# Expert matrices laid out with neighbouring rows in a partition, and transposes that read every 8th or 4th column

## The chip, the cores and the metric
The kernel runs on one core of a Trainium2 chip. The metric is the device time in microseconds of one execution; the time before is the median of three runs.

## What is computed
A decoder trunk of two layers on 512 tokens of 1024 features, all in fp32. A layer has a mixer (sliding-window attention and an mLSTM beside each other, from one input projection) and a mixture of 16 experts. The change touches the second part: the shift and scale before the experts, the router and the experts' matrices.

```python
for l in range(DEPTH):                                  # DEPTH = 2
    mod = c_act @ ada_w[l] + ada_b[l]
    sh1, sc1, g1, sh2, sc2, g2 = split(mod, 6)          # 1024 each
    ...                                                 # mixer, x = x + g1 * ...
    h2 = rms_norm(x, norm_ffn_w[l]) * (1.0 + sc2) + sh2
    scores = sigmoid(h2 @ router_w)                     # 16 experts, best group of 4, top 2 in it
    # per expert e, for the tokens routed to it:
    y = (silu(h @ w_gate[l, e]) * (h @ w_up[l, e])) @ w_down[l, e]   # 1024 -> 512 -> 1024
    x = x + g2 * (weighted sum of the two experts of a token)
```

## The kernel before
The five engines run their own instruction streams and meet in semaphores. In the loop over layers TensorE works through a fixed order of products (`group_order`), each into one of two PSUM banks that ScalarE and VectorE empty in turn. Then comes the expert stage.

Tokens are sorted by expert on the chip: their normalised rows are scattered into the DRAM buffer `expert_rows`, in blocks of 64 rows of one expert. The trace shows 22 blocks in layer 0 and 24 in layer 1. For every block b TensorE runs, in this order (loop at line 1199): gate/up products of block b+1 (`gate_up`, line 1160, 16 products in two passes, 32 matmuls); the transposes of the rows of block b+2 (`x_transposes`, line 1152, eight of 64 rows by 128 columns); the down product of block b (`down`, line 1172); the transposes of the hidden rows of block b+1 (`h_transposes`, line 1166, four). A transpose takes the tile `xg` or `hx` as TensorE's stationary operand and the identity as the moving one. ScalarE and VectorE apply scale and shift while they empty the x transposes (lines 800 and 1685, one value a partition from `A2` and `modc`), and VectorE writes a block's result to `yb` (1689), which ScalarE's queue stores in two DMAs (817).

An expert has 2 MB each of gate, up and down. Three buffers hold them. SyncE issues gate and up of expert e when the last gate/up product of expert e-3 is done (`load_expert`, lines 433 to 436, issues at 428 and 431), GpSimd issues down when its last down product is done (541 to 544). All matrix loads of SyncE go through one queue in order. The source of each is made by `of`: partition p receives rows p, p+128, p+256 and so on, each a run of 2 KB (gate, up) or 4 KB (down) in DRAM. TensorE's product number k takes rows 128k to 128k+127 and so needs in partition p the feature 128k+p; that is what `x_transposes` gives it, by reading columns 128k to 128k+127.

The same feature order serves the router: `h2T` (line 1114) transposes the normalised rows `xn`, `rwz` holds the router's matrix (line 395), `A2` and the columns 24 to 39 of `modc` hold scale and shift. These come from parts 6 to 9 of the `ada` product. For those VectorE sums eight weighted rows (`sum_mid`), and TensorE turns the sum of 512 columns into four PSUM columns (`column_sums`, line 865, called from 1095), between the products of `gb` and `yb`. Norm weight and bias for them are columns of `pc`, a transposed block of small parameters. `params` (lines 368 to 387) loads small parameters with 14 DMAs a layer, for layer 0 at the start ahead of `x` and three parts of `ada_w`, for layer 1 among the loads of layer 0's experts.

## Time and profile before

| | |
|---|---|
| median of 3 runs | 1733.24 us (1731.43 to 1737.04) |
| profiled execution, span from first to last instruction | 1724.8 us |
| TensorE busy | 1506.9 us, 87% of the span |
| VectorE, ScalarE, GpSimd busy | 563.9, 323.4, 121.8 us |
| mean granted clock of TensorE | 0.940 of full speed |
| moved by DMA | 366.59 MB in 160813 packets, mean 213 GB/s |
| queue q1 (SyncE) | 127568 packets, 256.26 MB |
| queue q0 (GpSimd) | 21664 packets, 83.89 MB |
| expert stages | about 540 to 846 us and 1380 to 1700 us |

How to read it: a line number stands for the instruction's line in the kernel. Times of instructions are in us or, where marked, ns; positions are us from the first instruction. PE is TensorE's matmuls, PEld its weight loads, DVE VectorE, ACT ScalarE, POOL GpSimd, SP SyncE; a q behind it means the engine's issuing side. Ends of matmuls are modelled. The DMA share is the mean busy share of the core's 16 DMA engines; it can come out a little above 1.

### The profile page before, as it was taken

What the parts mean: (1) busy time and instruction counts of PE and PEld (TensorE: products, weight loads), DVE (VectorE), ACT (ScalarE), POOL (GpSimd) and SP (SyncE); (2) the same over time, 40 slices, a digit from 0 to 9 for tenths busy, and PEclk for the clock granted to TensorE, in tenths of its full rate; (3) what the DMA queues carried; (4) which work ended last, traced back from release to release, by engine and by line L of the source; (5) the groups of instructions that cost most, each with busy time, mean ns of one, the idle gap of its engine ahead of it and who ended that gap; (6) DMA issues with size and microseconds to landing.
All of it is one profiled execution on the core that took longest, in us unless ns stands there. A gap on an engine that the chain in (4) does not pass through costs nothing.

```text
span 1724.8 us, 18335 instructions
## 1 busy us (share of the span) xinstructions
PE 1506.9 (87%) x5819; PEld 669.3 (39%) x5820; DVE 563.9 (33%) x1459; ACT 323.4 (19%) x809; POOL 121.8 (7%) x157
## 2 busy tenths in 40 slices
PE   4999999999983999987749999999999387999982
PEld 1544444544441333332335444454444132333330
DVE  1346432446333212111134554243642411221213
ACT  3133411200011212111132343111000121221210
POOL 1100000011101000000111000000110100000001
PEclk8999999999996999999769999999999789999996
DMA  9822111055747899999952111113563799997984
GB/s 307 338 97 98 49 49 49 13 206 173 291 142 268 268 375 379 376 388 360 322 180 98 49 49 50 49 49 108 206 224 145 292 314 381 378 354 247 310 303 165
DMA packets 160813, 366.59 MB, mean 213 GB/s; under 512 B 12433, under 2 KB 14705, under 8 KB 160753
## 3 DMA queue, kind: packets, MB, share of 16 engines
q1 hardware_dynamic: 127568, 256.26, 42.2%
q0 software_dynamic: 21664, 83.89, 12.8%
q10 hardware_dynamic: 11520, 25.70, 5.0%
q8 instruction: 31, 0.51, 0.1%
q14 instruction: 30, 0.24, 0.0%
HBM read 334.37 MB, written 31.46 MB: 212 GB/s over the span
## 4 chain that ended last, share of the span: by engine, by line
PE 69%; DMA 11%; SPq 5%; DVE 5%; issue 4%; ACT 2%; POOL 2%; ACTq 0%; DVEq 0%; POOLq 0%; PEldq 0%
PE bank L939 23%; PE bank L1160 14%; PE bank L929 11%; PE bank L1105 6%; PE bank L1172 6%; DMA weight_ring<-in_w_up_dram 6%; DMA regA<-in_w_up_dram 2%; SPq L428 2%; SPq L431 2%; SPq L371 2%; DMA weight_ring<-in_ada_w_dram 1%; PE bank L1152 1%; PE bank L999 1%; POOL expert_rows L558 1%; PE bank L988 1%
## 5 line engine op out<-in xcount | busy, mean ns | idle before, releaser
L939 PE MATMUL bank<-h_features,weight_ring 128*128 128x512 f32 x768 | 342.4, 599 | 3.1 <-ACT regB L674 1.9
L1160 PE MATMUL bank<-weight_ring,merged_features 128*64 128x512 f32 x960 | 227.2, 628 | 35.3 <-DMA weight_ring<-in_w_up_dram 28.2
L939 PEld LDWEIGHTS bank<-h_features,weight_ring 128*128 128x128 f32 x768 | 144.8, 192 | 182.7 <-issue 182.4
L929 PE MATMUL bank<-weight_ring,h_features 128*128 128x512 f32 (+1 forms) x512 | 196.1, 541 | 1.7 <-ACT h_features L628 1.7
L1703 DVE TENSOR_TENSOR merged_features<-bank,merged_features 64x512 f32<-64x512 f32 x44 | 30.5, 693 | 381.8 <-ACT merged_features L809 381.8
L1160 PEld LDWEIGHTS bank<-weight_ring,merged_features 128*64 128x64 f32 x960 | 73.5, 144 | 165.4 <-issue 160.8
L929 PEld LDWEIGHTS bank<-weight_ring,h_features 128*128 128x128 f32 x512 | 96.0, 190 | 97.0 <-issue 91.6
L1160 PE MATMUL bank<-h_features,merged_features 128*64 128x512 f32 x256 | 117.1, 612 | 11.0 <-DMA regA<-in_w_up_dram 10.0
L1160 PE MATMUL bank<-regA,merged_features 128*64 128x512 f32 x256 | 117.5, 614 | 0.0
L1105 PE MATMUL bank<-weight_ring,merged_features 128*128 128x512 f32 x256 | 110.4, 593 | 3.0 <-POOL merged_features L538 3.0
L1172 PE MATMUL bank<-weight_ring,merged_features 128*64 128x512 f32 x480 | 109.6, 598 | 1.6 <-DVE merged_features L1689 1.6
L809 ACT ACTIVATE merged_features<-bank 64x512 f32<-64x512 f32 x46 | 27.1, 589 | 367.9 <-PE bank L1160 367.9
L1152 PE MATMUL bank<-ident,merged_features 64*128 64x64 f32 x384 | 34.9, 233 | 44.5 <-DMA merged_features<-expert_rows 44.5
L800 ACT ACTIVATE merged_features<-bank,mod_cols,scale 128x64 f32<-128x64 f32 x192 | 61.9, 402 | 60.6 <-PE bank L1152 58.3
L1105 PEld LDWEIGHTS bank<-weight_ring,merged_features 128*128 128x128 f32 x256 | 48.5, 190 | 63.4 <-issue 60.2
L1544 DVE SCALAR_TENSOR_TENSOR regP<-weight_ring,c_padded,regP 128x512 f32<-128x512 f32 x84 | 63.2, 752 | 3.0
L1160 PEld LDWEIGHTS bank<-h_features,merged_features 128*64 128x64 f32 x256 | 34.8, 141 | 73.7 <-issue 73.7
L1685 DVE TENSOR_SCALAR merged_features<-bank,scale,mod_cols 128x64 f32<-128x64 f32 x192 | 52.8, 338 | 27.1 <-PE bank L1152 25.5
L1689 DVE TENSOR_TENSOR merged_features<-bank,g_rows 128x512 f32<-128x512 f32 x46 | 31.8, 692 | 89.8 <-PE bank L1172 78.9
L1152 PEld LDWEIGHTS bank<-ident,merged_features 64*128 64x128 f32 x384 | 28.2, 142 | 82.0 <-DMA merged_features<-expert_rows 44.7
L939 PE MATMUL bank<-regB,weight_ring 128*128 128x512 f32 x128 | 57.4, 594 | 1.6 <-DVE regB L1562 1.6
L939 PE MATMUL bank<-regA,weight_ring 128*128 128x512 f32 x128 | 57.6, 592 | 0.0
(304 smaller groups left out, 1376.1 us busy)
## 6 DMA issues: line engine op xcount, KB each, us to landing
weight_ring<-in_ada_w_dram SPq DMA_DIRECT2D x24, 2048.0 KB, 8.7
weight_ring<-in_w_gate_dram SPq DMA_DIRECT2D x22, 2048.0 KB, 21.1
weight_ring<-in_w_down_dram POOLq DMA_DIRECT2D x22, 2048.0 KB, 14.9
weight_ring<-in_w_up_dram SPq DMA_DIRECT2D x22, 2048.0 KB, 20.4
weight_ring<-in_w_in_dram SPq DMA_DIRECT2D x18, 2048.0 KB, 8.9
h_features<-in_w_gate_dram SPq DMA_DIRECT2D x10, 2048.0 KB, 17.4
regA<-in_w_up_dram SPq DMA_DIRECT2D x10, 2048.0 KB, 27.4
regB<-in_w_down_dram POOLq DMA_DIRECT2D x10, 1536.0 KB, 11.5
```

The lines of the kernel that those rows point to most:

```text
L371: sp.dma_start(dst, src).then_inc(params_in, 16)
L428: sp.dma_start(gate_w[p], of(w_gate, l, e)).then_inc(w_gu[p], 16)
L431: sp.dma_start(up_w[p], of(w_up, l, e)).then_inc(w_gu[p], 16)
L800: last = ac.activation(xT[:, k, :], ps[2][:, MB * k:MB * k + MB], ACT.Identity, scale=A2[:, k:k + 1], bias=modc[:, 24 + k:25 + k])
L929: ins = te.matmul(bank[:, 0:w], hT[:, k, P * i:P * i + P], wv[:, k, :], start=(k == 0), stop=(k == KD - 1))
L939: ins = te.matmul(bank[:, :], wv[:, k, c0:c0 + P], rhs[:, k, :], start=(k == 0), stop=(k == kn - 1))
L1105: ins = te.matmul(bank[:, :], merged[:, k, P * i:P * i + P], slot("wo", k // 4, 4, D)[:, k % 4, 512 * h:512 * h + 512], start=(k == 0), st ...
L1152: ins = te.transpose(ps[(2, 6)[k % 2]][:, MB * k:MB * k + MB], xg[p][:, P * k:P * k + P], ident[MB * p:MB * p + MB, MB * p:MB * p + MB])
L1160: ins = te.matmul(ps[3][64 * part:64 * part + 64, :], xT[:, k, :], w[:, k, :], start=(k == 0), stop=(k == KD - 1))
L1172: ins = te.matmul(ps[5][64 * half:64 * half + 64, :], hxT[:, k, :], down_w[p][k][:, 512 * half:512 * half + 512], start=(k == 0), stop=(k ...
L1544: link(ve.scalar_tensor_tensor(mid_sum, w[:, k, :], cz[:, k, 0:1], mid_sum, ALU.mult, ALU.add))
L1685: last = ve.tensor_scalar(xT[:, k, :], ps[6][:, MB * k:MB * k + MB], A2[:, k:k + 1], modc[:, 24 + k:25 + k], ALU.mult, ALU.add)
```

## The change
Partition p of an expert's gate and up tile now holds rows 8p to 8p+7, one run of 16 KB in DRAM, and of a down tile rows 4p to 4p+3, also 16 KB (for the third buffer 12 KB and 4 KB). Product k then takes the feature 8p+k (4p+k) in partition p. So the x transposes read columns k, k+8, k+16 and so on, and the hidden ones k, k+4 and so on. The scale and shift columns, the router's matrix and `h2T` follow the same order of features. Their parameters come straight from DRAM into a new tile `ffc` with three more small DMAs a layer, in runs of 32 bytes, and `column_sums_ffn` makes a part's sum with eight products of 64 columns (read with a step of 8) in place of four of 128.

```diff
+        ffc = sb("ffn_param_cols", [P, 3, KD])
...
-            return w.rearrange("l e (k p) f -> (l e) p k f", p=P)[bass.ds(l * E + e, 1)].rearrange("a p k f -> p (a k) f")
+            return w.rearrange("l e (p k) f -> (l e) p k f", p=P)[bass.ds(l * E + e, 1)].rearrange("a p k f -> p (a k) f")
...
+                rows(ffc[:, 0, :], lay(norm_ffn_w, l).rearrange("a (p k) -> p (a k)", p=P))
+                rows(ffc[:, 1, :], lay(ada_b, l)[:, 3 * D:4 * D].rearrange("a (p k) -> p (a k)", p=P))
+                rows(ffc[:, 2, :], lay(ada_b, l)[:, 4 * D:5 * D].rearrange("a (p k) -> p (a k)", p=P))
...
-            sp.dma_start(rwz[:, :, 0:E], router_w.rearrange("(k p) e -> p k e", p=P)).then_inc(const_in, 16)
+            sp.dma_start(rwz[:, :, 0:E], router_w.rearrange("(p k) e -> p k e", p=P)).then_inc(const_in, 16)
...
-                wait_head(pe, params_in, t, 14 * 16, 14 * 16)
+                wait_head(pe, params_in, t, 17 * 16, 17 * 16)
...
+            def column_sums_ffn(bank, rows, h):
+
+                for k in range(KD):
+                    ins = te.matmul(bank[64 * h:64 * h + 64, k:k + 1], rows.rearrange("q (p k) -> q k p", k=KD)[:, k, :], ones[:, 0:1], start=True, stop=True)
+                return ins
...
-                            ins = column_sums(bank, mid_sum)
+                            ins = column_sums_ffn(bank, mid_sum, c_ % 2)
...
-                        ins = te.transpose(bank[:, P * i:P * i + P], xn[:, i, P * k:P * k + P], ident[:, :])
+                        ins = te.transpose(bank[:, P * i:P * i + P], xn[:, i, :].rearrange("t (p k) -> t k p", k=KD)[:, k, :], ident[:, :])
...
-                        ins = te.transpose(ps[(2, 6)[k % 2]][:, MB * k:MB * k + MB], xg[p][:, P * k:P * k + P],
+                        ins = te.transpose(ps[(2, 6)[k % 2]][:, MB * k:MB * k + MB], xg[p].rearrange("t (p k) -> t k p", k=KD)[:, k, :],
...
-                        ins = te.transpose(ps[4][:, MB * k:MB * k + MB], hx[:, P * k:P * k + P], ident[0:MB, 0:MB])
+                        ins = te.transpose(ps[4][:, MB * k:MB * k + MB], hx.rearrange("t (p k) -> t k p", k=FC)[:, k, :], ident[0:MB, 0:MB])
...
-                        columns(j, bank, read, link)
+                        r, c0 = 64 * (j % 2), 24 if j < 8 else 32
+                        link(ve.tensor_copy(modc[r:r + 64, c0:c0 + KD], bank[r:r + 64, 0:KD]))
+                        ve.sem_inc(read, 1)
...
-                        link(ve.tensor_tensor(modc[:, 24:40], modc[:, 24:40], pc[:, 84:100], ALU.add))
-                        link(ve.scalar_tensor_tensor(A2[:, :], modc[:, 32:40], 1.0, pc[:, 8:16], ALU.add, ALU.mult))
+                        link(ve.tensor_tensor(modc[:, 24:40], modc[:, 24:40], ffc[:, 1:3, :].rearrange("p a k -> p (a k)"), ALU.add))
+                        link(ve.scalar_tensor_tensor(A2[:, :], modc[:, 32:40], 1.0, ffc[:, 0, :], ALU.add, ALU.mult))
```

## Rows read from the trace of the kernel before

**Rows 1.** the page, part 4: shares of the chain that ended last.
```profile
PE 69%; DMA 11%; SPq 5%; DVE 5%; issue 4%; ACT 2%; POOL 2%; ACTq 0%; DVEq 0%; POOLq 0%; PEldq 0%
```

**Rows 2.** TensorE's waits, 540 to 846 us: us in total, times, longest.
```profile
PE bank L1160 <- DMA weight_ring<-in_w_up_dram: 18.5, 3, 11.1
PE bank L1160 <- DMA regA<-in_w_up_dram: 5.6, 2, 4.5
```

**Rows 3.** the same, 1380 to 1700 us.
```profile
PE bank L1160 <- DMA weight_ring<-in_w_up_dram: 9.7, 2, 4.9
PE bank L1160 <- DMA regA<-in_w_up_dram: 4.4, 1, 4.4
```

**Rows 4.** stretches: length, busy us by engine, clock, DMA share, GB/s.
```profile
370.00:376.00 6.00, 6.00 (x15) 2.66 (x14) 3.14 (x4) 0.00 (x0) 2.53 (x2) 1.00 1.05 388
55.00:73.00 18.00, 18.00 (x56) 10.44 (x55) 4.22 (x13) 2.79 (x7) 1.97 (x1) 1.00 1.02 422
590.00:823.00 233.00, 208.44 (x1049) 77.65 (x1049) 44.73 (x108) 40.57 (x108) 11.16 (x16) 0.96 1.04 374
822.90:825.90 3.00, 3.00 (x8) 1.08 (x10) 0.00 (x0) 0.00 (x0) 0.00 (x0) 0.50 1.05 388
1409.00:1459.00 50.00, 40.60 (x202) 15.14 (x199) 9.93 (x24) 8.36 (x23) 3.57 (x5) 0.96 1.04 375
1460.00:1644.00 184.00, 183.58 (x944) 68.63 (x942) 37.72 (x91) 35.03 (x93) 6.35 (x9) 0.99 0.95 326
```

**Rows 5.** the chain in order of time: start, us, what.
```profile
18.35 20.28 DMA weight_ring<-in_ada_w_dram
...
715.64 9.83 PE bank L1160 x32
...
1675.62 9.40 PE bank L1160 x32
```

**Rows 6.** TensorE in order of time, one block of layer 0: start, us.
```profile
578.74 3.65 PE L1172 MATMUL bank<-weight_ring,merged_features 128*64 128x512 f32 x16
582.32 0.46 PE L1166 MATMUL bank<-ident,merged_features 64*128 64x64 f32 x4
582.71 7.09 PE L1160 MATMUL bank<-weight_ring,merged_features 128*64 128x512 f32 x32
589.73 0.71 PE L1152 MATMUL bank<-ident,merged_features 64*128 64x64 f32 x8
```

**Rows 7.** SyncE's issues in order of time: start, us that the issue took.
```profile
8.95 0.43 SPq L371 DMA_DIRECT2D qk_norm_rows<-in_q_norm_w_dram  x1
...
590.12 0.37 SPq L428 DMA_DIRECT2D weight_ring<-in_w_gate_dram  x1
...
760.84 10.65 SPq L428 DMA_DIRECT2D h_features<-in_w_gate_dram  x1
...
799.02 3.45 SPq L428 DMA_DIRECT2D weight_ring<-in_w_gate_dram  x1
...
1643.54 2.73 SPq L431 DMA_DIRECT2D weight_ring<-in_w_up_dram  x1
```

**Rows 8.** TensorE's weight loads in the block of rows 6.
```profile
578.10 0.57 PEld L1152 LDWEIGHTS bank<-ident,merged_features 64*128 64x128 f32 x8 [0.81 <-issue]
```

**Rows 9.** the page, part 5: busy us, mean ns of one.
```profile
L1689 DVE TENSOR_TENSOR merged_features<-bank,g_rows 128x512 f32<-128x512 f32 x46 | 31.8, 692 | 89.8 <-PE bank L1172 78.9
L1152 PEld LDWEIGHTS bank<-ident,merged_features 64*128 64x128 f32 x384 | 28.2, 142 | 82.0 <-DMA merged_features<-expert_rows 44.7
```

**Rows 10.** VectorE by shape, whole run: busy us, mean ns of one.
```profile
L1646 DVE TENSOR_REDUCE gate_weights<-regP 128x4 f32<-128x64 f32 x4 | 0.9, 220 | 0.1
...
L1630 DVE TENSOR_REDUCE regP<-regP 128x16 f32<-128x64 f32 x2 | 0.5, 265 | 0.1
```

**Rows 11.** TensorE in order of time: column sums, and transposes of h2T.
```profile
405.56 0.95 PE L865 MATMUL bank<-ones,regP 128*128 128x1 f32 x8
...
502.20 5.06 PE L1114 MATMUL bank<-ident,regA 128*128 128x128 f32 x24 [2.75 <-DVE regA L1586]
```

**Rows 12.** landing times of the stores of line 817.
```profile
DMA to landing us min/median/max: 2.3/6.3/7.4
```

## The prediction, made before the changed kernel ran

> **What bounds the kernel now.** I read the page's chain first: of what ended last 69% is TensorE and 11% DMA [rows 1]. So TensorE sets the end except where a transfer comes late. Next the list of TensorE's waits, for the two expert stages alone. Five gate/up products of layer 0 wait for `w_up`, 18.5 + 5.6 = 24.1 us [rows 2], and three of layer 1, 9.7 + 4.4 = 14.1 us [rows 3]. A wait leaves a second loss: the granted clock is 0.50 (1.2 GHz) in the 3 us after it [rows 4], and the 32 matmuls that follow take 9.83 or 9.40 us [rows 5] where they take 7.09 in a block that didn't wait [rows 6]. Third, the table by stretches [rows 4]. From 590 to 823 us the DMA engines are busy without a break (share 1.04) at 374 GB/s, and so from 1409 to 1459. From 1460 to 1644 they are not the limit: TensorE is busy 183.6 of 184 us. So layer 0 is bound by its transfers and layer 1, for the longer part, by TensorE. The change touches both: its loads may be faster, its transposes can hardly be.
>
> **Loads with 16 KB runs.** Gate and up are read in 2 KB packets, down in 4 KB packets. The trace has both sizes at a steady rate: 2 KB packets alone (`ada_w`, 370 to 376 us) move 388 GB/s, 4 KB packets alone (the zero fill of the row buffer, in the other direction, 55 to 73 us) 422 GB/s [rows 4]. No row shows 16 KB. The bounds are no gain, and a little above 422 (say 435), since the step from 2 to 4 KB gave 34 GB/s and further ones should give less. I take 422, the nearest row. Of layer 0 twelve experts' gate and up (numbers 4 to 15, issued from 590.12 to 799.02 and after [rows 7]), 12 x 4.19 = 50.3 MB, cross the saturated stretch: 129.6 us at 388, 119.2 us at 422, so 10.4 us less, 0.87 us an expert. Of layer 1 three experts (3, 4, 5) fall in such a stretch, 2.6 us, and the last one's own load gains 0.9.
>
> The sum does not use this: the Trainium skill, page "DMA: Bandwidth & Descriptors", section "Why small descriptors are slow (HBM only)", names a fixed overhead of about 3 cycles a packet. For 2 KB, 64 beats of 32 B, that is an estimated 4.5%, half of the 9% between my two rows; by it layer 0 would gain some 5 us in place of 10.4.
>
> SyncE is freed too: an issue of 1024 packets takes 0.37 us when the ring has room and 10.65 when it is full [rows 7]; one of 128 should stay short. I cost this at nothing. The engines are busy the whole time, so an earlier issue only lengthens the line.
>
> **Transposes with a step.** A transposed tile is TensorE's stationary operand, so what is read with a step is the weight load; the products' own operands stay contiguous. The eight loads of L1152 span 0.57 us [rows 8]; less the last one's own 0.142 [rows 9] that is 0.061 us from one to the next. What does a step of 16 or 32 bytes cost? No TensorE row has one. VectorE has: in the router a reduction over 64 elements in steps of 16 bytes (L1630) takes 265 ns, against 220 over 64 contiguous ones (L1646) [rows 10], 0.70 ns an element more. VectorE's plain rate is 692 ns for 512 elements, 1.35 each [rows 9], so as a ratio this is 1.5 and adds 32 ns to a weight load; as time, 128 x 0.70, it adds 90. The middle is a doubled load, +61 ns, which I take. Ends for the range: 0, and 142 (the whole printed duration once more). The first load of each group can be fetched under the matmuls before it, so 7 + 3 = 10 of a block's 12 are exposed: +0.61 us a block, where a block now takes 7.09 + 3.65 and its transposes some 0.9 [rows 6].
>
> A rule of the Trainium skill, page "SBUF — State Buffer", section "Door 1: The DMA port swizzle", says that memory is read in 16-byte lines and that a step is free up to 4 elements of fp32. By it the eight loads of `xg` (step 8) pay and the four of `hx` (step 4) don't. The VectorE row has a step of exactly 4 and is slower, so the trace speaks against the free step; by the rule a block would pay 0.43 us, and the sum would be some 3 us lower.
>
> **Expert stages, summed.** Layer 0: transfers -10.4. The saturated stretch starts when expert 1's last gate/up product frees its buffer, three blocks in, 3 x 0.61 = +1.8. After the last load has landed the last transposes add 0.4. TensorE's own path up to that landing has 24.1 us of waits and twice 2.7 of slow clock to lose (29.5) and 20 x 0.61 = 12.2 of work to gain, so the transfers still end last. Net **-8.2**. Layer 1: the early stretch -2.6 (TensorE has 4.9 + 4.4 us of slack there and uses 3.7). From 1459 to 1675 there are 18 blocks, +11.0. The last wait (4.8 us, before 1675.62) is for a load issued at 1643.54, when TensorE itself frees the buffer, three blocks earlier; so it shrinks by 0.9 + 1.8 = 2.7. Tail +0.4. Net **+6.1**.
>
> **The other transposes and the sums.** `h2T`: 64 loads over both layers, back to back, 24 in 5.06 us [rows 11]; 56 exposed x 61 ns = **+3.4** (0 to 8.0). `column_sums_ffn` has 8 products where `column_sums` had 4, each in two passes. 8 passes take 0.95 us now [rows 11], 0.119 each. The 16 passes load 64 columns each: half the time of 128 contiguous ones, the same if the step doubles it; so 16 x 0.119 = 1.90, +0.95 us. Nothing covers it (matmuls stand on both sides) and it runs 8 times: **+7.6** (3.7 with a free step).
>
> **Three more parameter loads.** At the start SyncE issues them ahead of `x` and three `ada` parts, and the chain runs along that queue into the load that ends at 38.6 us [rows 5]. 3 x (0.43 + 0.04) = **+1.4** [rows 7]; they move 4 KB each, nothing further. For layer 1 they are issued among the expert loads, long before TensorE asks. The re-laid router and VectorE's copies (8 columns for 4) keep their counts: nothing.
>
> **Sum.** -8.2 + 6.1 + 3.4 + 7.6 + 1.4 = +10.3 us. The profiled execution spans 1724.8 us; the median is 1733.24, so 8.4 us lie outside the span or between executions, and the change doesn't touch them. 1733.2 + 10.3 = **1743.5 us**, +0.6%.
>
> **Rivals.**
> *B, the step is free for TensorE.* For it: a weight load need not be fed as VectorE is. Against it: VectorE's row. Layer 0 -10.4, layer 1 -2.6 - 0.9, the sums +3.7, the start +1.4: -8.8, **1724.4 us**; with 435 GB/s another 5 less, 1719. This is the faster side.
> *C, a load with a step costs its printed 142 ns more.* A block pays 1.42. Layer 0: TensorE's path becomes the later one, -29.5 + 28.4 + 0.8 = -0.3; layer 1 -2.6 + 25.6 - 5.0 + 0.8 = +18.8; `h2T` +8.0, sums +12.9, start +1.4: +40.8, **1774.0 us**.
> *D, small row transfers starve behind 16 KB packets.* At 422 GB/s an engine takes 0.62 us for 16 KB. A store of a block's result is 8 packets an engine; it lands in 6.3 us median, 2.3 at least [rows 12]. If each packet waits for one of each weight queue it takes 8 x 1.24 + 2.3 = 12.2 us. The next result is there 11.7 us after this one and is wanted some 7 us later, so about 18 us are hidden. Only if bursts of eight go first (2 x 10 + 2.3 = 22 us) is TensorE held, up to 5 us a block; in half of layer 1's 18 bound blocks +45 on the forecast, **1789 us**.
> *E, the loads don't get faster.* The engines' share is 1.05 with 2 KB and 1.02 with 4 KB packets, so packets may not be the limit. Layer 0 +2.2, layer 1 +9.6, the rest +12.4: +24.2, **1757.4 us**.
>
> **How the numbers follow.** Forecast (step 32 to 90 ns, loads at 422): chance 0.43, with these ends +1.3 to +19.2, 1734.5 to 1752.4. B 0.26, C 0.10, D 0.05, E 0.11, anything else 0.05. A measurement of this kernel can tell about 0.3%, 5.2 us, from no change. Faster: B and a little of the rest, 0.29. Within: the forecast's low end and B's high end, 0.16. Slower: 0.55. The range takes in B and E and stops short of C: 1716 to 1771.
>
> **What would show it.** TensorE's rows: L1152 x8 grows from 0.71 us to about 1.1, L1166 x4 from 0.46 to 0.65, L865 in mid-layer from 0.95 for x8 to 1.9 for x16. The windows: saturated stretches above 374 GB/s, near 400; packets down from 160813 to about 93000; SyncE's issues of L428 and L431 under 1 us. Wrong would be: L1152 unchanged (B), L1689 or L1172 waiting for row stores (D), an unchanged rate (E).

## The result: slower, by more than forecast

| | before | after |
|---|---|---|
| median | 1732.34 us (4 runs, 1725.11 to 1737.04) | 1757.22 us (4 runs, 1746.71 to 1763.19) |
| ratio | | 1.0143, 95% interval 1.0116 to 1.0169 |
| profiled execution, span | 1724.8 us | 1761.6 us |
| packets of DMA | 160813 | 93325 |
| first gate/up product to last down product, layer 0 | 294.9 us | 293.9 us |
| the same, layer 1 | 308.0 us | 316.7 us |

The change costs 24.9 us; +10.3 was forecast. The direction held, but the cost is 2.4 times the forecast's. The profiled execution of after was the slowest of its four, 6 us above their median. That of before was quicker than its median: in the four executions of after the time is 1.6 us longer than the span, so a span of 1724.8 us stands for some 1726.4 us, 6 below the median. So the spans differ by 36.8 us. Of these 2.8 fall before the end of the first token's products, 7.9 before the first expert stage, -1.0 in it, 15.7 between the stages, 8.7 in the second, 2.7 behind it. In the chain of after there is a wait of 7.0 us between the layers, on work that the trace can't name, which the profiles of e1 to e5 don't have. Of the 15.7 us 4.3 come in that place (from the stage's last product to the next layer's first transposes TensorE takes 44.3 us for 40.0).

**Where the time ends now.** The page's chain of after, shares by engine, then its largest groups:

```profile
PE 72%; DMA 12%; DVE 5%; issue 4%; ACT 3%; POOL 2%; SPq 1%; ACTq 1%; another core or an unknown queue 0%; DVEq 0%; POOLq 0%; PEldq 0%
PE bank L949 23%; PE bank L1170 14%; PE bank L939 11%; DMA expert_rows<-merged_features 9%; PE bank L1182 7%; PE bank L1115 6%; PE bank L1162 2%; PE bank L1176 1%; DMA weight_ring<-in_ada_w_dram 1%; PE bank L1009 1%; POOL expert_rows L562 1%; PE bank L998 1%; DVE x_tokens L1728 1%; DMA expert_rows<-regA,slot_index 1%; SPq L372 1%
```

The DMA share is about that of rows 1, but it is another DMA: the weights are gone, and the stores of the blocks' results (`expert_rows<-merged_features`) hold 9%. TensorE's waits in the two stages of after (total us, times, longest) name no weight any more; rows 2 and 3 had 24.1 and 14.1 us for `w_up`. What they name is the down product (L1182, before L1172), in layer 0 and then in layer 1:

```profile
PE bank L1182 <- issue: 8.8, 3, 4.8
...
PE bank L1182 <- issue: 5.3, 1, 5.3
PE bank L1182 <- DVE merged_features L1701: 4.3, 1, 4.3
```

By the kernel's order it waits for a PSUM bank that VectorE has not emptied, because VectorE waits for its one result buffer; the trace names VectorE in the last of the three rows, and e3 below tests it. VectorE's waits for the stores, whole run, before and after:

```profile
DVE merged_features L1689 <- DMA expert_rows<-merged_features: 11.0, 2, 6.6
```
```profile
DVE merged_features L1701 <- DMA expert_rows<-merged_features: 154.3, 20, 13.8
```

And the chain of after in layer 0, pieces over 1.2 us: six stores in a row, 14.2 us in the mean. All 92 stores of after have a median of 8.6 us and a longest of 17.1, where rows 12 had 6.3 and 7.4:

```profile
695.25 14.74 DMA expert_rows<-merged_features
711.61 15.73 DMA expert_rows<-merged_features
728.97 13.49 DMA expert_rows<-merged_features
744.08 11.06 DMA expert_rows<-merged_features
756.76 13.18 DMA expert_rows<-merged_features
771.57 17.13 DMA expert_rows<-merged_features
```

**The rate.** Stretches of 100 us inside the saturated part of layer 0, before and then after (length; busy us of PE, PEld, DVE, ACT, POOL; clock, DMA share, GB/s):

```profile
600.00:700.00 100.00, 99.70 (x518) 37.21 (x516) 22.22 (x54) 20.25 (x54) 5.58 (x8) 1.00 1.04 379
700.00:800.00 100.00, 87.02 (x420) 31.73 (x416) 17.54 (x43) 15.95 (x43) 5.51 (x8) 0.93 1.05 379
```
```profile
600.00:700.00 100.00, 100.00 (x494) 38.83 (x492) 19.88 (x48) 18.09 (x48) 3.69 (x7) 1.00 1.00 376
700.00:800.00 100.00, 89.66 (x406) 35.80 (x404) 16.71 (x41) 15.82 (x42) 4.22 (x8) 0.91 1.01 389
```

379 GB/s became 376 and 389: 1% more in the mean, not the 9% taken. The landing times moved nevertheless (KB each, median us), gate and up first of before, then of after:

```profile
weight_ring<-in_w_gate_dram SPq DMA_DIRECT2D x22, 2048.0 KB, 21.1
weight_ring<-in_w_down_dram POOLq DMA_DIRECT2D x22, 2048.0 KB, 14.9
weight_ring<-in_w_up_dram SPq DMA_DIRECT2D x22, 2048.0 KB, 20.4
```
```profile
weight_ring<-in_w_down_dram POOLq DMA_DIRECT2D x22, 2048.0 KB, 15.1
weight_ring<-in_w_gate_dram SPq DMA_DIRECT2D x22, 2048.0 KB, 10.9
weight_ring<-in_w_up_dram SPq DMA_DIRECT2D x22, 2048.0 KB, 16.3
```

What gate and up gained, down lost. Counted from the first gate/up product of layer 0, the last `w_up` of that layer landed after 264.8 us in place of 276.5, and the last `w_down` after 276.3 in place of 265.3. The last weights of the layer came no earlier than before.

**The steps.** One block of after in order of time, to lay beside rows 6, and the weight loads of its x transposes, beside rows 8:

```profile
578.47 1.09 PE L1162 MATMUL bank<-ident,merged_features 64*128 64x64 f32 x8
579.50 3.65 PE L1182 MATMUL bank<-weight_ring,merged_features 128*64 128x512 f32 x16
583.08 0.69 PE L1176 MATMUL bank<-ident,merged_features 64*128 64x64 f32 x4
583.70 7.09 PE L1170 MATMUL bank<-weight_ring,merged_features 128*64 128x512 f32 x32
...
578.47 0.96 PEld L1162 LDWEIGHTS bank<-ident,merged_features 64*128 64x128 f32 x8 [0.81 <-issue]
```

0.71 + 0.46 became 1.09 + 0.69: +0.61 us a block, as forecast. The loads are (0.96 - 0.57) / 7 = 0.056 us further apart.

**The column sums.** TensorE in mid-layer of after, then the clock (the column before the DMA share) in the product behind a sum. Rows 11 had 0.95 us for a sum, the product behind it took 7.11:

```profile
420.99 2.08 PE L895 MATMUL bank<-ones,regP 128*64 128x1 f32 x16
423.00 8.83 PE L949 MATMUL bank<-h_features,weight_ring 128*128 128x512 f32 x16
...
423.00:426.00 3.00, 3.00 (x6) 1.49 (x6) 2.63 (x5) 0.00 (x0) 0.29 (x1) 0.66 0.52 132
426.00:429.00 3.00, 3.00 (x6) 1.11 (x5) 2.86 (x5) 0.00 (x0) 0.00 (x0) 0.77 1.04 406
```

### The profile page after: what moved, and what is told of

Same layout as the page of the kernel before. It is cut to its first block, busy times and chain, and to the rows that moved or that the text cites. A ratio compares the mean times of both kernels' runs of the same rounds, so it can differ in the third digit from the quotient of the medians.

```text
span 1761.6 us, 18469 instructions
## 1 busy us (share of the span) xinstructions
PE 1553.5 (88%) x5883; PEld 704.2 (40%) x5884; DVE 557.9 (32%) x1459; ACT 323.1 (18%) x809; POOL 114.5 (6%) x157
## 2 busy tenths in 40 slices
DMA packets 93325, 366.62 MB, mean 208 GB/s; under 512 B 13297, under 2 KB 15569, under 8 KB 80977
## 4 chain that ended last, share of the span: by engine, by line
PE 72%; DMA 12%; DVE 5%; issue 4%; ACT 3%; POOL 2%; SPq 1%; ACTq 1%; another core or an unknown queue 0%; DVEq 0%; POOLq 0%; PEldq 0%
PE bank L949 23%; PE bank L1170 14%; PE bank L939 11%; DMA expert_rows<-merged_features 9%; PE bank L1182 7%; PE bank L1115 6%; PE bank L1162 2%; PE bank L1176 1%; DMA weight_ring<-in_ada_w_dram 1%; PE bank L1009 1%; POOL expert_rows L562 1%; PE bank L998 1%; DVE x_tokens L1728 1%; DMA expert_rows<-regA,slot_index 1%; SPq L372 1%
## 5 line engine op out<-in xcount | busy, mean ns | idle before, releaser
L949 PE MATMUL bank<-h_features,weight_ring 128*128 128x512 f32 x768 | 350.0, 610 | 2.2 <-ACT regB L678 1.9
L1170 PEld LDWEIGHTS bank<-weight_ring,merged_features 128*64 128x64 f32 x960 | 69.6, 141 | 135.4 <-issue 130.5
L1182 PE MATMUL bank<-weight_ring,merged_features 128*64 128x512 f32 x480 | 113.6, 617 | 6.9 <-DVE merged_features L1701 4.3
L1170 PE MATMUL bank<-h_features,merged_features 128*64 128x512 f32 x256 | 113.2, 595 | 1.0 <-issue 1.0
L1170 PE MATMUL bank<-regA,merged_features 128*64 128x512 f32 x256 | 113.3, 595 | 0.0
L1701 DVE TENSOR_TENSOR merged_features<-bank,g_rows 128x512 f32<-128x512 f32 x46 | 31.8, 692 | 210.7 <-DMA expert_rows<-merged_features 154.3
L1162 PE MATMUL bank<-ident,merged_features 64*128 64x64 f32 x384 | 52.6, 279 | 45.6 <-DMA merged_features<-expert_rows 45.6
L1162 PEld LDWEIGHTS bank<-ident,merged_features 64*128 64x128 f32 x384 | 45.9, 200 | 83.1 <-DMA merged_features<-expert_rows 45.7
L1182 PE MATMUL bank<-regB,merged_features 128*64 128x512 f32 x192 | 51.2, 674 | 12.9 <-issue 12.8
## 6 DMA issues: line engine op xcount, KB each, us to landing
regB<-in_w_down_dram POOLq DMA_DIRECT2D x10, 1536.0 KB, 14.1
```

Of the source, the lines that this page charges most:

```text
L949: ins = te.matmul(bank[:, :], wv[:, k, c0:c0 + P], rhs[:, k, :], start=(k == 0), stop=(k == kn - 1))
L1162: ins = te.transpose(ps[(2, 6)[k % 2]][:, MB * k:MB * k + MB], xg[p].rearrange("t (p k) -> t k p", k=KD)[:, k, :], ident[MB * p:MB * p + M ...
L1170: ins = te.matmul(ps[3][64 * part:64 * part + 64, :], xT[:, k, :], w[:, k, :], start=(k == 0), stop=(k == KD - 1))
L1182: ins = te.matmul(ps[5][64 * half:64 * half + 64, :], hxT[:, k, :], down_w[p][k][:, 512 * half:512 * half + 512], start=(k == 0), stop=(k ...
L1701: ve.tensor_tensor(yb, ps[5][:, :], g2bc[:, :], ALU.mult).then_inc(y_taken, 1)
```

## The experiments
**Theory 1**: 16 KB packets move hardly more bytes; they change which queue waits, and starve the row stores; the steps cost 0.61 us a block; the stepped column sums cost their own time and the clock behind them. **Rivals**: rival E of the prediction as it stood (nothing but a rate that stays), the number of passes rather than the step as the price of the sums (3b below), the step alone as the cause, and a plain gain from the loads alone.

Each series had its own runs of the kernel before beside it: 1729.58 us for e1 to e4, 1730.31 for e5 to e8, 1732.05 for e9 to e12, where the runs of after had 1732.34. So a difference between two medians of different series is good to some us only; from the ratios e3, e4, e6 and e8 come out 17, 13, 16 and 33 us below after, for 18, 15, 16 and 37 from the medians.

### e1 and e2: the layout of after, smaller packets

```diff
-                    sp.dma_start(gate_w[p], of(w_gate, l, e)).then_inc(w_gu[p], 16)
+                    for k in range(KD):
+                        sp.dma_start(gate_w[p][:, k:k + 1, :], of(w_gate, l, e)[:, k:k + 1, :]).then_inc(w_gu[p], 16)
```
Up is cut alike, down goes in four DMAs with packets of 4 KB. e2 takes two rows at a time.

> The changed kernel with the same places for every row, but gate and up loaded in eight DMAs of 2 KB packets and down in four of 4 KB packets, as before the change. Theory 1 (the row stores starve behind 16 KB packets): VectorE's wait for row stores before its result row, 154 us in the changed kernel, falls back to about 11 us, no down product waits for it, and the gate/up products wait for w_up again, 35 to 50 us; the expert stages keep a block period of about 12.25 us. Time 1750 to 1760 us, since the transfers bind layer 0 again. Rival (the store path stalls for another reason, such as the longer block): VectorE's wait for stores stays above 100 us. Rival 2 (packet size changes nothing in the rate): the saturated stretch of layer 0 shows the same GB/s as in the changed kernel.

> The changed kernel with gate and up in four DMAs of 4 KB packets each and down in four of 4 KB packets; places unchanged. Theory 1: a store's packet waits for 4 KB per queue and not for 16, VectorE's wait for stores is under 30 us, the stalls of the down products in both layers (some 10 us a layer) are gone; weight waits are smaller than with 2 KB packets because the rate is nearer to 422 GB/s. Time 1740 to 1750 us. Rival (16 KB is better for the weights than it is bad for the rows): 1757 us or more.

e1: 1759.03 us, ratio to before 1.0158 (1.0117 to 1.0199). VectorE's waits for stores 154.3 to 12.1 us, and TensorE waits for `w_up` again, 33.8 us. e2: 1747.44 us, 1.0107 (1.0069 to 1.0145); stores 11.3, `w_up` 22.9. The rate at 600 to 800 us is 370 and 381 in e1, 382 and 385 in e2. So with 2 KB packets the weight waits are back and the store waits gone, as in the kernel before, and the time can't be told from that of after. That the big packets' gain is paid back in full is not shown: in the profiled executions the two stages together take 620.1 us in e1 and 610.6 in after. 4 KB is better than 2 KB (the slowest run of e2, 1753.01, is faster than the fastest of e1, 1756.17); against after its interval overlaps. The fall of the store waits needs smaller packets only, since every row has the place that it has in after.

### e3: two result buffers

```diff
-        yb = mflat[:, 3072:3584]
+        yb = [mflat[:, 3072:3584], mflat[:, 3584:4096]]
...
-                                act.dma_start(xd[bass.ds(b * MB, MB), 512 * h:512 * h + 512], yb[64 * h:64 * h + 64, :]).then_inc(y_out, 16)
+                                act.dma_start(xd[bass.ds(b * MB, MB), 512 * h:512 * h + 512], yb[p][64 * h:64 * h + 64, :]).then_inc(y_fly[p], 16)
```

> The changed kernel with two buffers for a block's result, so that VectorE waits for the store before last and not for the last one. 16 KB packets stay. Theory 1: VectorE's wait for stores almost vanishes, the down products follow without a gap, and each expert stage is some 10 us shorter: 1735 to 1745 us. Rival (the transfers as a whole are the limit, the stores only show it first): the gate/up products wait for w_up in place of that, and the time stays within 5 us of 1757.

1739.04 us, 1.0047 (1.0028 to 1.0066): 18 us less than after. The stage of layer 0 takes 286.8 us (after 293.9, before 294.9), that of layer 1 307.9 (316.7, 308.0).

```profile
DVE merged_features L1705 <- DMA expert_rows<-merged_features: 52.5, 10, 9.5
```

Nothing else was changed, so the late stores behind a single buffer are shown to cost this much. A third of VectorE's wait is left, but TensorE's gaps ahead of down products shrink from 18.4 us in after (8.8 and 9.6 in the two layers) to some 0.6.

### e4 and e6: the steps of xn and of the sums taken away
e4: VectorE writes the normalised rows in the new order, and the x and h2T transposes read without a step.

```diff
-                    ve.tensor_scalar(xn[:, i, :], xs[:, i, :], rs[:, 4 + i:5 + i], None, ALU.mult).then_inc(xn_ready, 1)
+                    ve.tensor_scalar(xn[:, i, :].rearrange("t (k p) -> t k p", k=KD), xs[:, i, :].rearrange("t (p k) -> t k p", k=KD), rs[:, 4 + i:5 + i], None, ALU.mult).then_inc(xn_ready, 1)
```

> The changed kernel, but VectorE writes the normalised rows in the new order of features (reading with a step of 8 there, 8 instructions in all), so that the transposes of xg and h2T read contiguous columns; only the four of hx keep their step. Theory 2 (a stepped weight load costs about 60 ns more): the eight transposes span 0.71 us again, the block period falls from 12.25 to about 11.85 us, and the time by 8 to 13 us to about 1747. Rival (the step is not what lengthened the block): the period stays at 12.25 and the time at 1757. If the stalls for stores depend on the block period, they grow by a part of what is gained.

1741.81 us, 1.0067 (1.0034 to 1.0099), 15 below after by the medians and 13 by the ratios. The block period is 11.87 us for 12.25, as expected, and VectorE's waits for stores grow to 177.4 us.

e6: VectorE's last addition of a column sum is written in the new order (`mid_perm`), and the eight products read it without a step.

```diff
-                    ins = te.matmul(bank[64 * h:64 * h + 64, k:k + 1], rows.rearrange("q (p k) -> q k p", k=KD)[:, k, :], ones[:, 0:1], start=True, stop=True)
+                    ins = te.matmul(bank[64 * h:64 * h + 64, k:k + 1], rows[:, 64 * k:64 * k + 64], ones[:, 0:1], start=True, stop=True)
```

> The changed kernel, but VectorE writes the last step of the weighted sum in the new order (one instruction per part reads with a step), so the eight products of the column sums read contiguous columns; their count stays. Theory 3a (the step lengthens them): 2.08 us fall to about 1.4 us, the clock stays up in the product group after them (7.1 us and not 8.8) and the time falls by 5 to 10 us to 1748 to 1752. Theory 3b (their number does, each pass having a fixed price near 0.12 us): they stay at 1.9 us or more, the clock still falls, and the time stays within 3 us of 1757.

1740.86 us, 1.0052 (1.0029 to 1.0075): 16.4 less than after. A sum of e6 with the product behind it, and its clock:

```profile
422.84 1.09 PE L896 MATMUL bank<-ones,regP 128*64 128x1 f32 x16
423.86 7.13 PE L950 MATMUL bank<-h_features,weight_ring 128*128 128x512 f32 x16
...
424.00:427.00 3.00, 3.00 (x8) 1.32 (x9) 2.78 (x4) 0.00 (x0) 1.14 (x1) 1.00 0.57 150
```

16 passes without a step take 1.09 us, with it 2.08, and the clock stays at 1.00 (2.4 GHz). So it is the step and not the number of passes. (A pass of these sixteen takes 64 columns, one of the eight before 128.)

### e5: down as before

```diff
-                        ins = te.transpose(ps[4][:, MB * k:MB * k + MB], hx.rearrange("t (p k) -> t k p", k=FC)[:, k, :], ident[0:MB, 0:MB])
+                        ins = te.transpose(ps[4][:, MB * k:MB * k + MB], hx[:, P * k:P * k + P], ident[0:MB, 0:MB])
...
-                        po.dma_start(ring[:, (2, 5)[p], :].rearrange("p (k n) -> p k n", k=FC), of(w_down, l, e)).then_inc(w_dn[p], 16)
+                        po.dma_start(ring[:, (2, 5)[p], :].rearrange("p (k n) -> p k n", k=FC), of_down(l, e)).then_inc(w_dn[p], 16)
```

> The changed kernel with down as before the change (4 KB packets, the transposes of hx without a step); gate and up keep 16 KB. Theory 1 in numbers: a row packet waits for 16 KB of one weight queue (0.62 us) and 4 KB of the other (0.16), so twelve of them (a row load and two stores share the queue) take 12 x 0.8 + 2.3 = about 12 us, below the 18 us that are hidden: VectorE's wait for stores under 60 us, no stall of the down products, 1740 to 1745 us with the four cheaper transposes (-4 us). Rival (one queue of 16 KB packets is enough to starve the rows): the wait stays over 100 us and the time over 1750.

1747.29 us, 1.0096 (1.0075 to 1.0117), above what was expected. VectorE waits 69.0 us for stores, less than 154.3 though more than the 60 expected, and they hold no down product. But a wait appears that neither kernel has, TensorE's for `w_down`:

```profile
PE bank L1186 <- DMA weight_ring<-in_w_down_dram: 24.0, 3, 12.1
PE bank L1186 <- DMA mlstm_v_and_one<-in_w_down_dram: 6.2, 2, 5.8
```

The 4 KB packets of GpSimd's queue now stand beside 16 KB ones of SyncE's, and down lands after 17.6 us (`weight_ring`) and 20.7 (`regB`) in place of 14.9 and 11.5.

### e9 and e10: each half of the change alone, on the kernel before
e9 changes `of` and nothing else; e10 changes the x and hidden transposes and nothing else. Both leave out the other half, so rows and features don't match in their products.

```diff
-            return w.rearrange("l e (k p) f -> (l e) p k f", p=P)[bass.ds(l * E + e, 1)].rearrange("a p k f -> p (a k) f")
+            return w.rearrange("l e (p k) f -> (l e) p k f", p=P)[bass.ds(l * E + e, 1)].rearrange("a p k f -> p (a k) f")
```
```diff
-                        ins = te.transpose(ps[(2, 6)[k % 2]][:, MB * k:MB * k + MB], xg[p][:, P * k:P * k + P],
+                        ins = te.transpose(ps[(2, 6)[k % 2]][:, MB * k:MB * k + MB], xg[p].rearrange("t (p k) -> t k p", k=KD)[:, k, :],
...
-                        ins = te.transpose(ps[4][:, MB * k:MB * k + MB], hx[:, P * k:P * k + P], ident[0:MB, 0:MB])
+                        ins = te.transpose(ps[4][:, MB * k:MB * k + MB], hx.rearrange("t (p k) -> t k p", k=FC)[:, k, :], ident[0:MB, 0:MB])
```

> The kernel before with the loads of the change alone: partition p of gate, up and down tiles gets neighbouring rows (16 KB packets); no transpose, no column sum, no parameter and no router column is changed. The rows of a tile then don't match the features they are multiplied with, so the experts' results aren't the reference's, and since layer 1 routes on what layer 0 made, layer 1 may have another number of blocks; layer 0 is comparable block by block. Theory 1 (16 KB packets raise the rate by only 2 to 3% and starve the row stores): a saturated rate of 385 to 390 GB/s, VectorE's waits for the store of the block result over 80 us in place of 11, a block period back at 11.7 us, stage of layer 0 285 to 293 us (before 294.9), whole kernel 1722 to 1735. Theory 2 (the loads alone are a plain gain and only the steps and sums cost): waits for stores under 30 us, stage of layer 0 under 286, whole kernel 1712 to 1720.

> The kernel before with the steps alone: the block transposes read their columns with a step of 8 and 4, every load, column sum, h2T and parameter stays as it was. The experts' results aren't the reference's, and layer 1 may have another number of blocks. If the steps cost what the rows of the changed kernel show (0.61 us a block) and nothing else: layer 0, bound by its transfers, +1 to +3 us (294.9 before), layer 1 +10 to +12 us (308.0 before, for 24 blocks), whole kernel 1740 to 1747, VectorE's waits for stores about 11 us, the saturated rate 375 to 380 GB/s. If the steps also disturb something further (the clock, the order of loads) the stages grow by more, 1750 and above. If the bound of layer 1 is elsewhere and hides them, 1730 to 1735.

e9: 1736.54 us, 1.0035 (1.0017 to 1.0053). Its layer 1 has 25 blocks, not 24, as VectorE's list there shows (busy us, mean ns, idle before):

```profile
L1689 DVE TENSOR_TENSOR merged_features<-bank,g_rows 128x512 f32<-128x512 f32 x25 | 17.3, 692 | 94.9 <-DMA expert_rows<-merged_features 68.1 <-PE bank L1172 26.9
```

A block is 11.65 us, so with 24 blocks e9 would be at some 1724.9, against 1732.05 of before in the same comparison: the loads alone are worth about -7 us. That is worked out, not measured. Layer 0, which has its 22 blocks, is measured: 289.9 us for 294.9. Layer 1 takes 316.3 with 25 blocks, so some 304.6 for 308.0. No product waits for weights, the rate at 600 to 800 us is 383 and 381, and

```profile
DVE merged_features L1689 <- DMA expert_rows<-merged_features: 184.7, 26, 14.3
```

Two down products of layer 1 show what a late store costs, the gap ahead of each and the slow clock in it (6.05 us, and 5.25 with the four matmuls that follow the second, for 3.65):

```profile
1447.14 6.05 PE L1172 MATMUL bank<-weight_ring,merged_features 128*64 128x512 f32 x16 [5.54 <-DVE merged_features L1689]
...
1479.47 4.39 PE L1172 MATMUL bank<-regB,merged_features 128*64 128x512 f32 x12 [6.26 <-issue]
```

So the plain gain of theory 2 falls, and the starvation needs no step. e10 has 22 and 24 blocks and took 1742.64 us, 1.0058 (1.0037 to 1.0079): +10.6. Layer 0 298.1 us (+3.2), layer 1 316.3 (+8.3), stores wait 11.3 us, the two transposes take 1.09 and 0.69. The whole and the steps are as expected, layer 1 a little less (10 to 12 was). TensorE waits 29.6 us for `w_up`, for 38.2 before.

### e7, e8, e11 and e12: what is left to win
e7 keeps down as before and gives gate and up two neighbouring rows a partition (4 KB packets in both queues, a step of 2).

```diff
-            return w.rearrange("l e (p k) f -> (l e) p k f", p=P)[bass.ds(l * E + e, 1)].rearrange("a p k f -> p (a k) f")
+            return w.rearrange("l e (k p j) f -> (l e) p k j f", p=P, j=2)[bass.ds(l * E + e, 1)].rearrange("a p k j f -> p (a k) j f")
```

> A middle way from the kernel before: gate and up with two neighbouring rows per partition (4 KB runs, features 256k + 2p + j), transposes of xg and h2T and the column sums with a step of 2 elements (8 bytes, two in each 16 bytes), four products per column sum, down unchanged. If the step's price comes from every element lying in another 16 bytes, a step of 2 is free: the eight transposes span 0.71 us, the block period is 11.7 and column sums 0.95 us. With packets of 4 KB the waits for w_up (38 us before) shrink by the 2 to 3% that the saturated rate rose in the changed kernel, some 5 to 8 us; three more small loads at the start cost 1.4. 1722 to 1730 us. Rival (any step costs): period 12.1 or more and 1745 us.

1726.49 us, 0.9977 (0.9963 to 0.999). VectorE waits 10.8 us for stores, TensorE 21.2 for `w_up`. The time is within what was expected, but not for its reason: in the transposes the step of 2 isn't cheaper than that of 8 (1.09), the block period is 12.09 us, and what makes up for it is a wait for `w_up` that shrank by 17 us where 5 to 8 were expected. In the column sums the same step of 2 cost nothing: eight passes take 0.99 us for 0.95, and the next product begins 1.09 us after the start of the sum (408.76 after 407.67), as before.

```profile
570.70 1.17 PE L1167 MATMUL bank<-ident,merged_features 64*128 64x64 f32 x8
```

e8 joins e3, e4, e5 and e6: 16 KB for gate and up, 4 KB for down, two result buffers, no step at all.

> The changed kernel with every cost taken out that was found: two result buffers, rows and sums written in the new order by VectorE so that no transpose or sum has a step, down as before (4 KB). Gate and up in 16 KB runs remain, and eight products in the column sums. If theories 1 and 2 hold the block period is 11.7 us again, VectorE hardly waits for stores, the waits for w_up are shorter than before the change, and what is left of the loss is the column sums and the start. 1722 to 1730 us. Rival (16 KB packets bring nothing for the weights, the rate being set elsewhere): waits for w_up as before, some 38 us, and 1735 us or more.

1720.39 us, 0.9953 (0.9935 to 0.9971), faster than both kernels. Stores hold nobody, but down does:

```profile
PE bank L1191 <- DMA weight_ring<-in_w_down_dram: 31.1, 3, 13.9
PE bank L1191 <- DMA mlstm_v_and_one<-in_w_down_dram: 5.3, 2, 4.4
```

e11 is e8 with down in 16 KB packets and the hidden step of 4; e12 is e7 with two result buffers and no step (VectorE writes rows and sums in the order of the pairs).

> The changed kernel with two result buffers, rows written in the new order by VectorE, and contiguous column sums, as in the combined kernel at 1720.4, but down in 16 KB packets and the hidden transposes with their step of 4. Theory: 4 KB packets of the down queue starve beside 16 KB ones of the other queue (TensorE waited 31 us for w_down there), and with 16 KB in both queues the waits for w_down fall under 10 us; against it stands a block that is 0.2 us longer, 46 x 0.2 = 9 us in all, of which layer 1 shows about 5. Result 1716 to 1726. If the waits for w_down stay at 20 us or more, the size of the packets is not why, and the time is 1724 or more.

> Two neighbouring rows in a partition (4 KB packets in both queues), two result buffers, and no step in any transpose: VectorE writes the rows in the pair order, and writes the last addition of the column sums in it too, so column sums are the four products of before. Theory: the pairs kernel (1726.5) loses its 0.37 us a block and its stepped h2T, at most 15 us on TensorE's path in layer 1 and little in layer 0, which its transfers bind at 386 GB/s; stores have 4 KB packets beside them and wait about 11 us. So 1712 to 1721, below the combined kernel's 1720.4; a block period of 11.65 to 11.75 us. If small packets of loads were not the point and 16 KB ones give more rate, it stays at 1722 or above.

e11: 1723.88 us, 0.9951 (0.9932 to 0.9971); no wait for `w_down`, 9.6 us for `w_up`. e12: 1722.04 us, 0.9951 (0.9934 to 0.9968); the transposes take 0.71 and 0.46 again, `w_up` is waited for 32.5 us. I had set 1721 as its upper end. e8, e11 and e12 can't be told apart by their intervals. Two result buffers in the kernel before, and nothing else, were not tried; its VectorE waits 11.0 us for stores in all.

## Why the prediction was off, point by point
Two steps failed. The transfers were given a gain from a rate that didn't come, and what they took from the stores was left at nothing; and the column sums were given 7.6 us where they cost 12.9. The forecast's +10.3 can be split by part, and each part now has a measured or worked-out size:

| part | forecast | found | from |
|---|---|---|---|
| faster transfers | -13.9 | about -7 | e9, less one block |
| steps in the blocks | +11.8 | +10.6 | e10 |
| column sums | +7.6 | +12.9 | order of time of after; e6 |
| `h2T` | +3.4 | +1.3 | order of time of after |
| start | +1.4 | +2.8 | spans |
| sum | +10.3 | +20.6 | measured: +24.9 |

Each run's median is good to 2 or 3 us, and e3, e4 and e6 overlap (18, 15 and 16 us below after make 49, and e8, which joins them, is 37 below), so this is an account and no proof. The halves also act on each other: in the two stages e9 and e10 together come to -1.8 and +4.9 us, where after has -1.0 and +8.7. About what the sum lacks is in that, and no run says how.

**Transfers: the step that failed first.** The step "I take 422, the nearest row" took the rate of a write of zeros for that of a read in larger packets. For the rate the bound "no gain" was nearly right: 379 before, 376 and 389 after, 383 and 381 in e9. By the rate alone some 1 of the 10.4 us of layer 0 would be left. Gate and up did land 11.7 us earlier in layer 0, but down and the stores landed later for it, and this price the forecast put at nothing. Where a second result buffer takes most of it away, in e3, the stages are 8.1 and 0.1 us shorter than before, steps included; the forecast had 8.2 shorter and 6.1 longer. That layer 0 meets its number there is luck, since its rate didn't come. The figure of the Trainium skill, page "DMA: Bandwidth & Descriptors", section "Why small descriptors are slow (HBM only)", from which I had an estimated 4.5%, was nearer than my two rows, and still too high for the 1% from before to after.

What the packets did change is who waits. By size of packet (gate and up / down), waits in us for `w_up`, for `w_down`, and VectorE's for a store: 2/4 KB 38.2, 0, 11.0 (before) and 33.8, 0, 12.1 (e1); 4/4 KB 22.9, 0, 11.3 (e2) and 21.2, 0, 10.8 (e7); 16/16 KB 0, 0, 154.3 (after) and 0, 0, 184.7 (e9); 16/4 KB 0, 30.2, 69.0 (e5). The queue with the smaller packets loses, whichever it is, while the bytes a second change by 2 or 3% at most. Queues that take turns by packet would do this; that reading fits all seven and was not measured by itself. With two result buffers and no step e12 (4/4 KB) waits 32.5 us for `w_up`, so how much of the 38.2 the packets alone account for stays open.

**Rival D was real and had a chance of 0.05.** Of the three signs of being wrong that the prediction named, its own and E's unchanged rate came. Its sum had a store of 8 packets with turns of 1.24 us, 12.2 us, hidden under some 18. The stores of the chain took 11.1 to 17.1 us. The load of a later block's rows goes through the same queue of ScalarE and was left out of the count: 256 KB are 4 more packets an engine, 12 x 1.24 + 2.3 = 17.2, at the edge of the cover. (That the row load is what made the difference was argued, not tried.) The price was then less than D's 5 us a block: by the order of time of after, gaps of 10.2 us in layer 0 and 10.0 in layer 1 (18.4 of them ahead of down products, the rest ahead of gate/up), and 7.0 and 3.7 us of slow clock in the products behind. Together 31 us. In the kernel before the weight waits made 38.2 us and the slow clock behind them 13.0 (7.6 and 5.4), 51 in all. So of the 51 us that went, 31 came back under another name; less 20 us and plus 46 x 0.61 = 28 us of steps make +8, and the spans of the stages show +7.7.

**Column sums.** The step "8 passes take 0.95 us, 0.119 each" priced a pass and let the step only double it. 16 passes without a step take 1.09 us (e6), so halving the columns of a pass all but pays for doubling their number, and the step costs 0.99 more, 0.06 a pass. From the start of a sum to the next product it is 1.09 us before and 2.01 after; the fourth sum of a layer was followed by a wait of 1.5 us, which covers it (2.44 us before, 2.36 after). So the sums themselves cost 6 x 0.92 less 0.2, 5.4 us, less than the 7.6 forecast. The rest is what I had at nothing: behind two of a layer's four sums the clock falls (0.66 and 0.77 in the rows above), and the product takes 8.83 us for 7.11: the group that it belongs to takes 12.26 us for 10.54, and the next sum begins 1.8 us later, 4 x 1.8 = 7.3. From its first sum to the product behind its fourth a layer takes 43.27 us for 36.84, twice 6.43 = 12.9 in all; in e6 it takes 36.91. That e6 was 16 us faster than after in all is 3 more than this.

**Steps in the blocks: right.** 0.61 us a block forecast and found; a weight load is 56 ns further from the next (61 taken). That the price came so near is in part luck: it was the middle of two readings of VectorE's row, and the two rows of that pair differ also in what they write, 16 results and 4 (rows 10).

The trace spoke against the rule of a free step of up to 4 fp32 elements (the Trainium skill, page "SBUF — State Buffer", section "Door 1: The DMA port swizzle"), and the runs do too for the block transposes: `hx`, step 4, went from 0.46 to 0.69 us, and a step of 2 in e7 cost as much as one of 8. In e7's column sums the step of 2 was free, as by the rule.

**h2T** was over-priced, and its step can't be read at all. From the group before it to the one behind it the time is 10.2 us in both layers before, and 11.25 and 10.49 after. The first two rows below are of after, layer 0; most of the second is granted a clock of 0.50. The two behind are of e10, layer 1, whose `h2T` has no step: at the same clock the 24 take the same. Rows 11 too stood partly at a slow clock (0.68 and 0.50 from 502 to 506 us).

```profile
511.56 1.16 PE L1124 MATMUL bank<-ident,regA 128*128 128x128 f32 x8 [2.75 <-DVE regA L1598]
513.18 6.02 PE L1124 MATMUL bank<-ident,regA 128*128 128x128 f32 x24 [0.46 <-DVE h_features L1601]
```
```profile
1347.76 1.09 PE L1114 MATMUL bank<-ident,regA 128*128 128x128 f32 x8 [2.74 <-DVE regA L1586]
1349.32 6.01 PE L1114 MATMUL bank<-ident,regA 128*128 128x128 f32 x24 [0.47 <-DVE h_features L1589]
```

**Start.** The three issues cost what was said, 1.34 us:

```profile
10.36 0.43 SPq L372 DMA_DIRECT2D ffn_param_cols<-in_norm_ffn_w_dram  x1
10.83 0.91 SPq L372 DMA_DIRECT2D ffn_param_cols<-in_ada_b_dram  x2
```

The other 1.4 us stay open, and so small a difference can't be told from chance: the first column sum starts at 405.6 us before and 408.5 after, but at 405.8 in e2 and 406.1 in e3, which issue the same three loads. The tail is 2.7 us longer in after, 3.0 in e9 and 4.0 in e2, and no longer in e5 and e7.

**Rival E named 1757.4 us, and 1757.2 was measured.** That is mostly chance. Its rate was right. It then had +11.8 us in the two stages, where the spans show 7.7, and +12.4 elsewhere, where the parts above give some 17. It had neither the stores nor the clock behind the sums.

**SyncE.** As foreseen nearly all its issues of gate and up fell to 0.33 to 0.7 us (the last two of layer 0 took 2.12 and 1.20), and the forecast costed this at nothing; no run tests it by itself. The 8.4 us that the forecast put outside the span come mostly from a profiled execution that was quicker than the median; 1.6 us lie outside. The sum doesn't hang on it.

## What to carry to other kernels
Before you give a faster transfer a price, ask whether the row it rests on moves in the same direction; a larger packet may move hardly more bytes and still make every other queue wait, so look for the small transfer with a single buffer behind it and give it a second one. A step in what TensorE loads is paid in every load, in the transposes here some 0.05 us each, and behind the column sums it was paid again in the clock of what followed: let the engine that writes the tile anyway write it in the order in which it will be read. Split a change into its halves on the old kernel; here they were -7 and +11, and the total alone said neither.

## What the runs showed of the chip
- In the stretches at 600 to 700 and 700 to 800 us, packets of 16 KB in both queues moved 376 to 390 GB/s (after, e3, e4, e6, e9, e11), 4 KB 381 to 388 (e2, e7, e12), and 2 KB beside 4 KB 370 to 381 (before, e1, e10).
- With 16 KB packets in two queues a store of the block results landed after 8.6 us in the median and 17.1 at most (after; 17.7 in e9, 31.1 in e3, where two blocks' stores can be on their way), in the kernel before after 6.3 and 7.4 (rows 12). The longest was 9.4 in e2 and 8.0 in e12, with 4 KB.
- With 16 KB packets in both queues the last `w_up` of layer 0 landed 11.7 us earlier and the last `w_down` 11.0 later than with 2 and 4 KB (after and before), at nearly the same sum of bytes.
- In transposes of 64 rows a step in a weight load's columns cost about as much for 2, 4 and 8 elements: eight transposes took 1.17 us (2) and 1.09 (8) for 0.71, four 0.69 (4) for 0.46, so 0.05 to 0.06 us each. In column sums a step of 8 cost 0.06 us a pass (e6 against after) and a step of 2 nothing on TensorE's way (e7).
- Behind sixteen passes of one column with a step the product group was granted a mean clock of 0.86 in two of a layer's four cases (0.66 in the first stretch of 3 us). Behind the same sixteen without it (e6, 1.09 us for 2.08) it stayed at 1.00 in seven of eight cases; in the eighth, the last of layer 1, the group took 56.9 us for 55.2, and so it did in e12, with eight passes.
